# Gated delta-rule scan: state and output products in two alternating places, the query's product with the state moved behind the attention product

## The chip, the cores and the metric

The kernel runs on one core of one Trainium2 chip. The metric is the device time of one launch in microseconds, as a median over runs. All data are fp32. TensorE (PE in the profile) runs every fp32 matmul as two passes, so that one `nc.tensor.matmul` of the program shows as two MATMUL records and two LDWEIGHTS records.

## The reference, cut to what matters

The program computes two model blocks, one after the other: an RG-LRU layer followed by a gated DeltaNet layer, and then a layer with a long convolution and a state-space branch. The change touches the scan of the DeltaNet layer alone. Its recurrence over the chunks of a sequence is:

```
def step(state, inp):
    w_c, u_c, attn_c, q_c, k_c, e_c = inp
    v_new = u_c - einsum('bhcd,bhde->bhce', w_c, state)
    o_c = einsum('bhcd,bhde->bhce', q_c, state) + einsum('bhcm,bhme->bhce', attn_c, v_new)
    state = state * e_c[..., None, None] + einsum('bhcd,bhce->bhde', k_c, v_new)
    return state, o_c
```

There are 8 heads, 1024 tokens, and head size 128. Each chunk needs the state that the chunk before it left.

## The kernel before

The kernel cuts the 1024 tokens into 8 chunks of 128 (`NCH = 8`), so that every product of the scan is one 128x128x128 matmul. The 8 heads run one after the other: seven in a hardware loop, in which the threshold of each semaphore wait is computed in a register, and the last one written out behind it. A head first flips keys and queries, builds and inverts a triangular matrix for each chunk, and then scans its 8 chunks. While it does, TensorE also computes the four input projections of the next head ("fill" matmuls, 128x512, line 1279); in the last head the fills are the output projection of the heads that are done (line 1349).

The order is written by hand, one program for each engine; each engine takes its instructions strictly in that order and waits on semaphores. Within a chunk c these steps matter, named as in the code:

- **read** (PE, line 1447): keys times state, into place 0 of `R4`.
- **recall** (PE, line 1452, it has no mark of its own before): queries times state, into place 4 of `R5`.
- **delta** (DVE, line 1860): values minus the decayed read, into `delta[:, 0]`. It waits for read.
- **new** (PE, line 1455): the inverse times delta, into place 4 of `R4`. ACT copies it, scaled, to `delta[:, 1]` (line 1583).
- **mem** (PE, line 1459): keys times new, into place 0 of `R5`. DVE adds it to the decayed state and writes `memory` (line 1869).
- **o** (PE, line 1461): attention times new, into place 4 of `R4`, which new has used before. ACT copies it, scaled, to `o_tok` (line 1586); DVE then adds the scaled recall to it (line 1872; the tile is `part` or `part0` in the records).

One fill matmul stands between recall and new, and one between new and mem (two each in the last head). `R4` lies in PSUM banks 4 and 5 and `R5` in banks 6 and 7: places 0 to 3 of each in the first bank, 4 to 7 in the second. On DVE the order is: state of chunk c (1869), output of chunk c (1872), delta of chunk c + 1 (1860). In some chunks one more DVE instruction of 128x512 comes in: a join of projection products (line 1719) behind delta, and in the last head a sum (line 1732) ahead of delta. `memory` is one 128x128 tile before the change. Recall of chunk c + 1 waits until DVE and ACT are done with the output of chunk c, since it overwrites place 4 of `R5`.

When a head's scan is over, TensorE runs 4 more fills, flips the normed output (line 1370), runs the first 4 fills of the next head and flips its keys (line 1370 again), for which it waits for DVE's last step of the head (`y`, line 1889).

## Time and profile before

| what | value |
|---|---|
| median of 3 runs | 2160.57 us |
| lowest and highest run | 2154.43 and 2162.94 us |
| span of the profiled execution | 2150.7 us |
| PE busy in that span | 2070.0 us (96%) |
| DVE busy | 1364.1 us (63%) |
| ACT busy | 642.5 us (30%) |
| heads of the DeltaNet layer (from about 434 to 1191 us) | seven of 84.1 us and the last |

The profiled execution is one more execution, and its own device time is not among the three listed; its span runs from its first to its last instruction. The median of the runs lies 9.9 us above the span (2160.57 - 2150.7); what lies around the span is in that difference. The rows give start times in us from the span's start, and durations. A matmul's record includes the time in which its result drains while the next one already streams, so a start-to-start distance, not the duration, is what it costs in a row of matmuls.

### The profile page before, as it was taken

The numbers are of one execution on the slowest core, as the hardware profiler recorded it, in microseconds if no ns is written. First come the engines' busy times: TensorE is split into PE (matmuls) and PEld (weight loads), VectorE is DVE, ScalarE is ACT, GpSimd is POOL, SyncE is SP. The second block draws the span as 40 slices with busy tenths as digits, with TensorE's granted clock in tenths as the row PEclk, the third lists the DMA queues.
The fourth block names the chain that finished last, engine by engine and source line by source line (L and its number), as shares of the span: only waits on it lengthen the run. The fifth ranks groups of instructions, "written<-read, shape, count | busy, mean of one in ns | idle before, by whom it ended". The sixth has DMA issues, their size and how long they took to land. (4 is left out here: it accounts for less than half of the span.)

```text
span 2150.7 us, 20753 instructions
## 1 busy us (share of the span) xinstructions
PE 2070.0 (96%) x6898; PEld 1060.6 (49%) x6898; DVE 1364.1 (63%) x1918; ACT 642.5 (30%) x1063; POOL 234.5 (11%) x188
## 2 busy tenths in 40 slices
PE   6999999999999999999899899999999999999998
PEld 5444444446555556566555445554444444444443
DVE  4687753265746746647652578529999997534633
ACT  4345431323443434434311521012321111241021
POOL 0000001112212113122100400001000000003200
PEclk8999999999999999999999999999999999999999
DMA  9333389241111111111420316269722222334021
GB/s 342 110 109 100 116 272 236 89 92 35 47 29 37 38 37 37 24 36 43 147 41 1 108 59 120 74 189 250 173 59 75 68 73 69 103 103 137 20 98 59
DMA packets 243824, 207.17 MB, mean 96 GB/s; under 512 B 52204, under 2 KB 202785, under 8 KB 243745
## 3 DMA queue, kind: packets, MB, share of 16 engines
q1 hardware_dynamic: 213393, 157.25, 24.5%
q0 software_dynamic: 13056, 42.99, 8.2%
q10 hardware_dynamic: 17312, 6.10, 1.2%
q8 instruction: 38, 0.62, 0.1%
q14 instruction: 25, 0.20, 0.0%
HBM read 182.55 MB, written 60.33 MB: 113 GB/s over the span
## 5 line engine op out<-in xcount | busy, mean ns | idle before, releaser
L2300 PE MATMUL bank<-hT,ring 128*128 128x512 f32 x576 | 254.2, 592 | 0.0
L2300 PE MATMUL bank<-resid,ring 128*128 128x512 f32 x432 | 191.3, 592 | 0.0
L2300 PEld LDWEIGHTS bank<-hT,ring 128*128 128x128 f32 x576 | 109.5, 190 | 137.7 <-issue 136.7
L1279 PE MATMUL bank<-hT,ring 128*128 128x512 f32 x336 | 157.7, 595 | 1.8 <-ACT silu_z L1515 1.8
L3220 DVE SCALAR_TENSOR_TENSOR yT<-s_arena,yT 128x1024 f32<-128x1024 f32 x120 | 153.8, 1282 | 0.0
L3220 DVE SCALAR_TENSOR_TENSOR s_arena<-s_arena 128x1024 f32<-128x1024 f32 x112 | 143.5, 1282 | 0.0
L2272 PE MATMUL bank<-hT,ring 128*128 128x512 f32 x320 | 139.4, 594 | 0.0
L2300 PEld LDWEIGHTS bank<-resid,ring 128*128 128x128 f32 x432 | 82.1, 190 | 103.3 <-issue 102.3
L1869 DVE SCALAR_TENSOR_TENSOR memory<-memory,col_exp_last,bank 128x128 f32<-128x128 f32 x64 | 22.3, 348 | 153.7 <-PE bank L1459 153.7
L2272 PEld LDWEIGHTS bank<-hT,ring 128*128 128x128 f32 x320 | 60.2, 190 | 73.7 <-issue 73.4
L2345 PE MATMUL bank<-ssm_y,ring 128*128 128x512 f32 x192 | 83.4, 592 | 0.0
L1279 PEld LDWEIGHTS bank<-hT,ring 128*128 128x128 f32 x336 | 58.4, 191 | 49.9 <-issue 49.4
L1279 PE MATMUL bank<-resid,yT 128*128 128x512 f32 x168 | 82.5, 593 | 0.0
L2669 ACT ACTIVATE s_arena<-bank 128x512 f32<-128x512 f32 x54 | 32.2, 596 | 130.1 <-PE bank L2300 124.8
L640 PE MATMUL bank<-hT,ring 128*128 128x512 f32 x144 | 63.4, 595 | 0.3 <-DVE lru_arena L865 0.3
L1583 ACT ACTIVATE delta<-bank,gdn_stat 128x128 f32<-128x128 f32 x64 | 23.5, 367 | 128.5 <-PE bank L1455 128.5
L1349 PE MATMUL bank<-hT,yT 128*128 128x512 f32 x128 | 60.0, 593 | 0.0
L2345 PEld LDWEIGHTS bank<-ssm_y,ring 128*128 128x128 f32 x192 | 36.5, 190 | 45.9 <-issue 45.4
L3173 DVE TENSOR_TENSOR s_arena<-bank,s_arena 128x512 f32<-128x512 f32 x36 | 24.8, 688 | 53.6 <-PE bank L2300 53.6
L2595 PE MATMUL bank<-resid,s_arena 128*128 128x512 f32 x128 | 56.5, 593 | 1.1 <-DVE yT L3451 1.1
L685 PE MATMUL bank<-ada,yT 128*128 128x512 f32 x128 | 55.8, 593 | 0.7 <-issue 0.7
L685 PE MATMUL bank<-lru_arena,yT 128*128 128x512 f32 x128 | 56.1, 592 | 0.0
(585 smaller groups left out, 3671.7 us busy)
## 6 DMA issues: line engine op xcount, KB each, us to landing
ada<-in_ada_w SPq DMA_DIRECT2D x8, 2048.0 KB, 8.1
ring<-in_gdn_in_w SPq DMA_DIRECT2D x32, 512.0 KB, 4.1
ring<-in_w_in SPq DMA_DIRECT2D x54, 256.0 KB, 2.9
ab_U_sums<-in_w_in POOLq DMA_DIRECT2D x6, 2048.0 KB, 19.0
resid<-in_x SPq DMA_DIRECT2D x8, 1024.0 KB, 8.9
ring<-in_lru_in_w SPq DMA_DIRECT2D x16, 512.0 KB, 3.9
ring<-ab_U_sums SPq DMA_DIRECT2D x32, 256.0 KB, 3.0
lru_arena<-in_ada_w SPq DMA_DIRECT2D x6, 1024.0 KB, 12.5
```

Of the source, the lines that this page charges most:

```text
L640: last = nc.tensor.matmul(bank[:, to, :], w[:, k, :], v[:, k, :], start=(first and k == 0), stop=(k == KB - 1), skip_group_check=not (firs ...
L685: last = nc.tensor.matmul(bank[:, OUT_BANK[i], :], yT[:, k, t * P:(t + 1) * P], out_w[c][:, k, :], start=(k == 0), stop=(k == KT - 1))
L1279: last = nc.tensor.matmul(bank[:, to, :], w[:, k, :], v[:, k, :], start=(first and k == 0), stop=(k == KB - 1), skip_group_check=not only)
L1349: last = nc.tensor.matmul(bank[:, n % 4, :], yT[:, k, t * P:(t + 1) * P], w, start=(k == 0), stop=(k == KT - 2))
L1583: hd_act.mark(act.activation(delta[:, 1, :], R4[:, 4, :], ACT.Copy, scale=stat[:, 5, c:c + 1]), f"new{c}")
L2272: last = nc.tensor.matmul(bank[:, 2 * PAIR[name] + h, :], w[:, k, :], src[:, k, h * HALF:(h + 1) * HALF], start=(k == 0), stop=(k == kt - 1))
L2300: last = nc.tensor.matmul(bank[:, to, :], w[:, k, :], src[:, k, :], start=(start and k == 0), stop=(k == HK - 1), skip_group_check=not alone)
L2345: last = nc.tensor.matmul(bank[:, 2 * SINGLE_BANKS[name] + h, :], w[:, k, :], ssm_y[:, k, h * HALF:(h + 1) * HALF], start=(k == 0), stop=( ...
L2595: last = nc.tensor.matmul(bank[:, to, :], x[:, k, m, :], w[:, k, :], start=(start and k == 0), stop=(k == HK - 1), skip_group_check=not alone)
L2669: act_b.mark(act.activation(place, bank[:, PAIR_BANKS[name][2 if n == 2 else 0], :], ACT.Copy), f"{name}_kept{n}")
L3173: dve_b.mark(TT_(place, other, place, ALU.add), f"{name}_" + ("C11", "C12", None, "C22")[which])
L3220: dve_b.mark(dve.scalar_tensor_tensor(out=acc, in0=padded[:, p, j:j + S], scalar=taps[:, p, j:j + 1], in1=acc, op0=ALU.mult, op1=ALU.add), ...
```

## The change

`memory` becomes two tiles: chunk c reads `memory[:, c % 2]`, and the new state is written to `memory[:, (c + 1) % 2]`. The attention product o goes to place 5 or 6 of `R4` by turns, and recall to place 4 or 5 of `R5`. Recall is issued behind o, at the end of its chunk, and has a mark of its own. PE waits ahead of o for ACT's copy of the output of chunk c - 2, and ahead of recall for DVE's output step of chunk c - 2 (both only from c = 2 on); the wait for chunk c - 1 ahead of recall is gone. DVE waits for recall ahead of its output step.

```diff
-            memory = sb("memory", [P, P], scope)
+            memory = sb("memory", [P, 2, P], scope)
@@ PE
-                            hd_pe.mark(nc.tensor.matmul(R4[:, 0, :], kT[:, c, :], memory[:, :], start=True, stop=True), f"read{c}")
-                            if c:
-                                hd_dve.wait(pe, f"o{c - 1}", h)
-                                hd_act.wait(pe, f"o{c - 1}", h)
-
-                            nc.tensor.matmul(R5[:, 4, :], qT[:, c, :], memory[:, :], start=True, stop=True)
+                            hd_pe.mark(nc.tensor.matmul(R4[:, 0, :], kT[:, c, :], memory[:, c % 2, :], start=True, stop=True), f"read{c}")
                             fill(1, 2)
...
-                            hd_pe.mark(nc.tensor.matmul(R4[:, 4, :], attnT[:, c, :], delta[:, 1, :], start=True, stop=True), f"o{c}")
+                            if c >= 2:
+                                hd_act.wait(pe, f"o{c - 2}", h)
+                            hd_pe.mark(nc.tensor.matmul(R4[:, 5 + c % 2, :], attnT[:, c, :], delta[:, 1, :], start=True, stop=True), f"o{c}")
+                            if c >= 2:
+                                hd_dve.wait(pe, f"o{c - 2}", h)
+                            hd_pe.mark(nc.tensor.matmul(R5[:, 4 + c % 2, :], qT[:, c, :], memory[:, c % 2, :], start=True, stop=True), f"recall{c}")
@@ DVE
-                            hd_dve.mark(dve.scalar_tensor_tensor(out=memory[:, :], in0=memory[:, :], scalar=cols["exp_last"][:, h, c:c + 1],
+                            hd_dve.mark(dve.scalar_tensor_tensor(out=memory[:, (c + 1) % 2, :], in0=memory[:, c % 2, :], scalar=cols["exp_last"][:, h, c:c + 1],
                                                                  in1=R5[:, 0, :], op0=ALU.mult, op1=ALU.add), f"mem{c}")
+                            hd_pe.wait(dve, f"recall{c}", h)
                             hd_act.wait(dve, f"o{c}", h)
```

On TensorE, in the loop's heads, this is a stretch from the end of one chunk into the next before the change (names: `ck` keys, `cq` queries, `memory` state, `delta` the vectors, `buf_c` the inverse, `attnT` attention; L1279 is a fill):

```order
L1459 MATMUL bank<-delta,k_rest 128x128 [waits gdn_dve,gdn_act]
L1461 MATMUL bank<-delta,attnT 128x128
L58 REGISTER_ALU
L1447 MATMUL bank<-memory,ck 128x128 [waits gdn_dve]
L58 REGISTER_ALU
L58 REGISTER_ALU [waits gdn_dve]
L1452 MATMUL bank<-memory,cq 128x128 [waits gdn_act]
L1279 MATMUL bank<-resid,yT 128x512
L58 REGISTER_ALU
L1455 MATMUL bank<-delta,buf_c 128x128 [waits gdn_dve]
```

And the same stretch after it, from chunk 2 on:

```order
L1454 MATMUL bank<-delta,k_rest 128x128 [waits gdn_dve,gdn_act]
L58 REGISTER_ALU
L1458 MATMUL bank<-delta,attnT 128x128 [waits gdn_act]
L58 REGISTER_ALU
L1461 MATMUL bank<-memory,cq 128x128 [waits gdn_dve]
L58 REGISTER_ALU
L1447 MATMUL bank<-memory,ck 128x128 [waits gdn_dve]
L1279 MATMUL bank<-resid,ring 128x512
L58 REGISTER_ALU
L1450 MATMUL bank<-delta,buf_c 128x128 [waits gdn_dve]
```

The query's product stands ahead of the key's product now, and nothing is left between the key's product and the fill; two waits stand between the mem product and the query's product.

On DVE, from the state of one chunk to the delta of the next, one waiting instruction is new, ahead of the output step:

```order
 L1869 SCALAR_TENSOR_TENSOR memory<-memory,col_exp_last,bank 128x128
 L58 REGISTER_ALU
-L1872 SCALAR_TENSOR_TENSOR part<-bank,gdn_stat,part 128x128 [waits gdn_act]
+L58 REGISTER_ALU [waits gdn_pe]
+L1873 SCALAR_TENSOR_TENSOR part<-bank,gdn_stat,part 128x128 [waits gdn_act]
 L58 REGISTER_ALU
 L1860 ISA [waits gdn_pe]
```

The delta step still stands behind the output step.

## Rows read from the trace of the kernel before

**Rows 1.** The page: busy us and shares; clock in 40 slices; one group, idle before it

```profile
PE 2070.0 (96%) x6898; PEld 1060.6 (49%) x6898; DVE 1364.1 (63%) x1918; ACT 642.5 (30%) x1063; POOL 234.5 (11%) x188
...
PEclk8999999999999999999999999999999999999999
...
L1869 DVE SCALAR_TENSOR_TENSOR memory<-memory,col_exp_last,bank 128x128 f32<-128x128 f32 x64 | 22.3, 348 | 153.7 <-PE bank L1459 153.7
```

**Rows 2.** PE's waits, whole span: its longest line; us in total, times, longest us

```profile
PE bank L1447 <- DVE memory L1869: 16.6, 56, 0.3
```

**Rows 3.** Timeline of PE, loop's first head: start us, us, engine line tiles [idle before]

```profile
515.82 0.39 PE L1452 MATMUL bank<-memory,cq 128*128 128x128 f32 x2
516.04 1.02 PE L1279 MATMUL bank<-resid,yT 128*128 128x512 f32 x2
...
517.98 0.39 PE L1459 MATMUL bank<-delta,k_rest 128*128 128x128 f32 x2
518.20 0.39 PE L1461 MATMUL bank<-delta,attnT 128*128 128x128 f32 x2
518.90 0.49 PE L1447 MATMUL bank<-memory,ck 128*128 128x128 f32 x2 [0.31 <-DVE memory L1869]
519.51 0.48 PE L1452 MATMUL bank<-memory,cq 128*128 128x128 f32 x2
519.83 1.02 PE L1279 MATMUL bank<-resid,yT 128*128 128x512 f32 x2
520.69 0.38 PE L1455 MATMUL bank<-delta,buf_c 128*128 128x128 f32 x2
...
521.77 0.38 PE L1459 MATMUL bank<-delta,k_rest 128*128 128x128 f32 x2
```

**Rows 4.** Timelines of DVE and ACT in the same stretch

```profile
518.50 0.35 DVE L1869 SCALAR_TENSOR_TENSOR memory<-memory,col_exp_last,bank 128x128 f32<-128x128 f32 x1 [2.04 <-PE bank L1459]
519.03 0.35 DVE L1872 SCALAR_TENSOR_TENSOR part<-bank,gdn_stat,part 128x128 f32<-128x128 f32 x1 [0.18 <-ACT part L1586]
519.55 0.35 DVE L1860 SCALAR_TENSOR_TENSOR delta<-bank,col_neg_exp_g,v_tok 128x128 f32<-128x128 f32 x1 [0.18 <-PE bank L1447]
...
518.63 0.37 ACT L1586 ACTIVATE part<-bank,gdn_stat 128x128 f32<-128x128 f32 x1 [0.94 <-PE bank L1461]
```

**Rows 5.** Timeline of the second head: a weight load released by delta; a wait already met

```profile
600.20 0.35 DVE L1860 SCALAR_TENSOR_TENSOR delta<-bank,col_neg_exp_g,v_tok 128x128 f32<-128x128 f32 x1 [0.69 <-PE bank L1447]
600.61 0.19 PEld L1455 LDWEIGHTS bank<-delta,buf_c 128*128 128x128 f32 x1 [0.28 <-DVE delta L1860]
...
607.38 0.48 PE L1452 MATMUL bank<-memory,cq 128*128 128x128 f32 x2
...
607.70 1.02 PE L1279 MATMUL bank<-resid,ring 128*128 128x512 f32 x2
```

**Rows 6.** Timelines of PE and DVE, last head, one chunk into the next

```profile
1150.76 0.39 PE L1459 MATMUL bank<-delta,k_rest 128*128 128x128 f32 x2
...
1151.59 0.49 PE L1447 MATMUL bank<-memory,ck 128*128 128x128 f32 x2 [0.22 <-DVE memory L1869]
1152.27 0.49 PE L1452 MATMUL bank<-memory,cq 128*128 128x128 f32 x2 [0.20 <-DVE part L1872]
...
1152.73 0.35 DVE L1860 SCALAR_TENSOR_TENSOR delta<-bank,col_neg_exp_g,v_tok 128x128 f32<-128x128 f32 x1
```

**Rows 7.** Timelines of PE and DVE from a scan's end to the next head's keys

```profile
553.47 1.09 PE L1370 MATMUL bank<-ident,ck 128*128 128x128 f32 x8 [0.62 <-DVE yT L1889]
...
548.08 4.14 DVE L1658 SCALAR_TENSOR_TENSOR ck<-qkv_padded,vecs,ck 128x1024 f32<-128x1024 f32 x3
552.14 1.28 DVE L1889 SCALAR_TENSOR_TENSOR yT<-bank,vecs,silu_z 128x1024 f32 x1
```

**Rows 8.** PE ahead of the last head; then busy by window, with granted clock

```profile
1058.10 1.94 PE L1370 MATMUL bank<-ident,ck 128*128 128x128 f32 x8 [4.14 <-DVE yT L1889]
...
1056.00:1063.00 7.00, 4.90 (x23) 4.93 (x24) 7.00 (x6) 4.48 (x5) 3.24 (x1) 0.52 1.01 353
```

More of the change, by code:

```diff
@@ L1023, in block_program @@
             o_tok, o_normed = part0[:, :, :], AT
-            memory = sb("memory", [P, P], scope)
+            memory = sb("memory", [P, 2, P], scope)
             delta = sb("delta", [P, 2, P], scope)
             g_rows = delta[0:HEADS * NCH, 0, :]
-            fold_ab = memory[:, 0:2 * HEADS]
+            fold_ab = memory[:, 0, 0:2 * HEADS]
             g_dram = nc.dram_tensor("g_scratch", (HEADS * NCH, P), F32, kind="Internal").ap()
@@ L1041, in block_program @@
                           + [n for s in levels for n in halves(f"Y{s}") + (["v_flip"] if s == levels[0] else []) + halves(f"YT{s}") + (halves(f"F{s}") if s < 64 else [])]
-                          + [f"{n}{c}" for c in range(NCH) for n in ("read", "new", "mem", "o")] + ["o_flip"])
+                          + [f"{n}{c}" for c in range(NCH) for n in ("read", "new", "mem", "o", "recall")] + ["o_flip"])
             hd_act = Steps(sem("gdn_act"), ["k_sq", "decay", "q_silu", "q_sq", "k_rms", "v_silu"]
@@ L1585, in body @@
                             hd_pe.wait(act, f"o{c}", h)
-                            hd_act.mark(act.activation(o_tok[:, c, :], R4[:, 4, :], ACT.Copy, scale=stat[:, 1, c:c + 1]), f"o{c}")
+                            hd_act.mark(act.activation(o_tok[:, c, :], R4[:, 5 + c % 2, :], ACT.Copy, scale=stat[:, 1, c:c + 1]), f"o{c}")
                             if c:
@@ L1855, in body @@
                                 add_parts(7 + n, 8 + n)
-                        hd_pe.wait(dve, f"o{NCH - 1}", h, back=1)
-                        hd_dve.mark(dve.memset(memory[:, :], 0.0), "mem_zero")
+                        hd_pe.wait(dve, f"recall{NCH - 1}", h, back=1)
+                        hd_dve.mark(dve.memset(memory[:, 0, :], 0.0), "mem_zero")
                         for c in range(NCH):
@@ L1868, in body @@
                             hd_pe.wait(dve, f"mem{c}", h)
-                            hd_dve.mark(dve.scalar_tensor_tensor(out=memory[:, :], in0=memory[:, :], scalar=cols["exp_last"][:, h, c:c + 1],
+                            hd_dve.mark(dve.scalar_tensor_tensor(out=memory[:, (c + 1) % 2, :], in0=memory[:, c % 2, :], scalar=cols["exp_last"][:, h, c:c + 1],
                                                                  in1=R5[:, 0, :], op0=ALU.mult, op1=ALU.add), f"mem{c}")
+                            hd_pe.wait(dve, f"recall{c}", h)
                             hd_act.wait(dve, f"o{c}", h)
-                            hd_dve.mark(dve.scalar_tensor_tensor(out=o_tok[:, c, :], in0=R5[:, 4, :], scalar=stat[:, 3, c:c + 1],
+                            hd_dve.mark(dve.scalar_tensor_tensor(out=o_tok[:, c, :], in0=R5[:, 4 + c % 2, :], scalar=stat[:, 3, c:c + 1],
                                                                  in1=o_tok[:, c, :], op0=ALU.mult, op1=ALU.add), f"o{c}")
```

## The prediction

> **What bounds the kernel now.** I read the page first: PE is busy 96% of the span, and its clock reads 9 (90% or more) in all slices but the first [rows 1]. So time goes only if a hole in PE's stream goes, or PE gets less work; the change leaves PE its 5 small matmuls in each chunk. The second view is the list of PE's waits [rows 2]: its longest line is the key's product "read" (L1447), held 56 times by the state that DVE writes. 56 is 8 heads times chunks 1 to 7. But 16.6 us is not the whole hole, because a record covers the draining of a result. The whole is seen in start-to-start distances in the timeline [rows 3]. From mem to mem a chunk of the loop takes 521.77 - 517.98 = 3.79 us: mem to read 0.92, read to recall 0.61, recall to fill 0.32, fill to new 0.86, new to mem 1.08, which is new's 0.22 and the second fill's 0.86. A small matmul that follows another without a hole costs 0.22 (mem to o), so the distances 0.92, 0.61 and 0.32 hold the holes: 0.92 is mem and o (0.22 each) and 0.48 of waiting for DVE's state; 0.61 is read and 0.39 of waiting; 0.32 is recall and 0.10 of a start after a pause.
>
> Who releases recall? DVE's output step of the chunk before ends at 519.03 + 0.35 = 519.38, 0.13 ahead of recall at 519.51 [rows 3, 4]. DVE's state ends at 518.85, 0.05 ahead of read. So two releases follow each other: the state first, which the recurrence needs, and then the output step, which only frees a place in PSUM. In the last head the same pair is plain: read 1151.59, recall 1152.27, held by the output step [rows 6].
>
> **The change, part by part.**
>
> *Recall leaves the place between read and fill.* The wait for the output step of chunk c - 1 goes with it. The first fill can then start behind read alone. Read starts after a pause, as recall did, so I take recall's own distance to the fill for it: 0.32 (519.51 to 519.83). The distance from read to fill falls from 0.61 + 0.32 to 0.32.
>
> *Recall joins the end of its chunk.* Mem, o and recall now take 3 x 0.22 = 0.66, and read can't start until 0.92 after mem, since it waits for the state. The 0.48 hole takes recall's 0.22 in; 0.26 of it is left. In the last head the state is there 1151.59 - 1150.76 = 0.83 after mem [rows 6], still later than 0.66. So the recurrence sets read's start, as before, and recall there costs nothing.
>
> *New distance from mem to mem:* 0.92 + 0.32 + 0.86 + 0.22 + 0.86 = 3.18 instead of 3.79, **0.61 less**. In the last head read to recall is 1152.27 - 1151.59 = 0.68, and that goes.
>
> *What is late next.* With the first fill earlier, new could find its delta missing. Against the start of mem (517.98), delta runs from 1.57 to 1.92 [rows 4]. It is held by the end of read (0.92 + 0.49 = 1.41) and by DVE's output step (to 1.40) alike, and neither moves. The fill ends, and new can start, at 0.92 + 0.32 + 0.86 = 2.10. A weight load that delta releases comes 0.06 after delta's end (600.61 against 600.20 + 0.35) and takes 0.19 [rows 5]: 1.92 + 0.06 + 0.19 = 2.17. So new is between 0 and 0.07 late. I take 0: where the load was bare ahead of recall the matmul's second pass was only 0.10 behind its usual place, and with the load at 1.98 that fits into 2.10. The upper end, 0.07 in 49 chunks, is 3.4 us and goes into the range. In the last head two fills stand there, 1.72 us, and delta, even behind a sum, ends at 1153.08, 2.32 after mem; the fills last to 0.83 + 0.32 + 1.72 = 2.87. Nothing is late there.
>
> *Chunk 0* had no wait ahead of recall: 515.82 to 516.04, 0.22 [rows 3]. It moves from ahead of delta's path to the chunk's end and then fills the hole ahead of read 1. That is 0.22 less in each head. New of chunk 0 is ready for it: in the second head the load at 600.61 ends at 600.80, and the fill, 0.22 earlier than now, at about 600.77: 0 to 0.03 late.
>
> *Chunk 7* has no next read. Its recall puts 0.22 between o and the 4 fills at the head's end. Behind these PE waits 0.62 for DVE's last step `y` at the next head's keys, and DVE reaches `y` (552.14) straight out of its taps (548.08 to 552.22) [rows 7]; that chain starts at o, which recall follows. So the 0.22 comes out of the 0.62 in seven heads, and costs 0.22 in the last, where other work follows. Uncovered everywhere it would be 1.8 us.
>
> *The added waits.* PE's waits for chunk c - 2 are long met: DVE's output step of that chunk ended over one whole chunk earlier. What a met wait costs shows in two neighbours: recall to fill is 0.32 without a wait ahead of the fill (519.51, 519.83), and 607.70 - 607.38 = 0.32 with one [rows 3, 5]. So 0; the bound above is the 0.26 that is left ahead of read: only beyond it does a wait cost anything. DVE's new wait for recall has delta of chunk c + 1 queued behind it, and PE's new waits for that. Recall ends at 0.44 + 0.39 = 0.83 after mem; DVE's output step starts at 1.05, held by ACT's copy (0.65 to 1.02) [rows 4]. ACT is still last by 0.2.
>
> The Trainium skill, "Advanced Engine Details and Errata", Network/Comms, states 50 to 100 ns for a sequencer's reading of a semaphore. By it the two waits ahead of recall would put it up to 0.2 later, and the sum would shrink; the rows with a met wait show no such cost. This rule is the source of a rival below.
>
> *The state in two tiles* adds no instruction; DVE's state step keeps its shape (0.35). That PE reads one tile while DVE reads the same and writes the other is new in this trace: recall's two passes stream from 0.44 to 0.66, DVE's state step runs from 0.52. Bound: nothing below, since neither can get shorter; above, recall behind the whole state step, 0.43 later.
>
> *Sum:* 7 heads x 7 chunks x 0.61 = 29.9; last head 7 x 0.68 = 4.8; chunk 0, 8 x 0.22 = 1.8; last head's end, -0.22. Together **36.3 us**. The span goes from 2150.7 to 2114.4. The profiled execution's own device time isn't known; the runs' median lies 9.9 above its span, and I keep that: **2124.3 us**, 1.7% less.
>
> Outside the scan nothing else should answer. The weight loads for the next head are issued from points inside the fills and move with them; DVE idles 153.7 us ahead of its state steps alone, released by mem [rows 1], so it has room.
>
> **The rivals.**
>
> *A, a smaller gain: delta is late.* DVE's output step is held by recall instead of ACT, and delta behind it. Say each of the two added waits costs 0.1: recall then ends at 1.03, DVE starts 0.14 later (as the state step does: mem ends 518.37, DVE 518.50), at 1.17 instead of 1.05; delta ends at 2.04, its load at 2.29, and new is 0.19 late. That holds for the deltas behind chunks 2 to 6: 7 x 5 x 0.19 = 6.7 less, 2131. With recall held behind the whole state step (the 0.43 above), recall would end at 1.26, DVE's step start at 1.40, delta end at 2.27, its load at 2.52 and new 0.42 late: 49 chunks with 0.42 less, 20.6 us, 2145. The rows with a met wait speak against the first, and against the second only that both engines worked beside each other elsewhere. Chance of something from 2130 to 2146: 0.13.
>
> *B, no gain: the heads are paced by something else.* If DVE's chain at a head's end, or a load, did not move with the scan, PE's wait ahead of the keys (0.62) would grow by the 4.5 us that each head saves, and only the last head's gain would stay: 2156. Against it: DVE's chain follows the last chunk's output without a hole, and in the scan DVE idles most of the time. Chance of something from 2146 to 2171: 0.06.
>
> *C, slower: the output step of DVE becomes the scan's pace.* The place is the new DVE wait ahead of L1873. New may come 0.61 later than I say before a chunk is as long as it is now, that is, with DVE's output step at 1.05 + 0.54 = 1.59 (delta ends at 2.46, its load at 2.71); from there each 0.1 us costs 5.6 us over 56 chunks. It would need recall to end beyond 1.45 after mem instead of 0.83, and beyond 1.65 for 0.5% slower. In the trace no 128x128 matmul pair lasts over 0.49. Chance 0.03.
>
> *D, the clock.* PE's longest pause in the heads, 4.14 us ahead of the last one, is followed by a granted clock of 0.52, so mostly the 1.2 GHz level: the key flip takes 1.94 instead of 1.09 [rows 7, 8], 0.85 us more, and other work of that stretch likewise. After the change such pauses lie 30 us earlier; the fall can stay, go, or come at another pause. Both ways it is 1 to 3 us. The Trainium skill, "TensorE: Matmul & The Clock Gate", Part 1, says that how many matmuls run slow varies from run to run. No case of its own; it widens the others.
>
> **How the numbers follow.** Forecast (gain 30 to 38 us): 0.78; A: 0.13; B: 0.06; C: 0.03. The forecast's own range is 2116 to 2130: 2124.3, minus 2 for the clock and 6 for the spread of the runs (the lowest lies 6.1 below the median), plus 3.4 for the late new and 2 for the clock. To leave no more than 2 in 10 out I reach into A: 2115 to 2140. About 0.5% (10.8 us) is what a measurement of this kernel can tell from no change. Faster by more: 0.78 + 0.13 = 0.91 (both end below 2149.8); within: B's 0.06; slower: C's 0.03.
>
> **What would show it.** In the changed kernel's timeline: read to fill 0.32 where 0.93 was; mem to read still 0.92 (0.83 in the last head), with recall inside; mem to mem 3.18 in the loop and 4.8 in the last head; chunk 0 to chunk 1 0.22 shorter; the DVE output step released by ACT, not PE; the wait at the keys 0.4 instead of 0.62; each head of the loop 4.5 shorter. Delta's load late against the fill's end would show as a new line "L1450 held by DVE delta" in PE's waits. I am wrong if mem to read grows, if delta starts later than 1.57 after mem, or if the wait at the keys grows.

## The result, and the profile after

The changed kernel takes **2121.73 us** (median of 4 runs, 2120.38 to 2122.89); beside it, on the same chip, the kernel before takes 2157.82 (4 runs, 2154.43 to 2162.94). The ratio is 0.9838, 95% interval 0.982 to 0.9857: 36.1 us less, where 36.3 were forecast. One execution of the experiment e3 (5611 us) and one of the kernel before beside it (12333 us) were far slower than all others of their kernels and are left out of the medians and ratios below.

The page after. It answers to [rows 1]: busy us of each engine, and the group of DVE's state steps with its idle time.

```profile
PE 2058.8 (97%) x6898; PEld 1055.5 (50%) x6898; DVE 1364.1 (64%) x1918; ACT 642.7 (30%) x1063; POOL 235.3 (11%) x188
...
L1869 DVE SCALAR_TENSOR_TENSOR memory<-memory,col_exp_last,bank 128x128 f32<-128x128 f32 x64 | 22.2, 347 | 117.0 <-PE bank L1454 117.0
```

The instructions are the same in number (6898 on PE, 1918 on DVE). What fell is waiting: DVE's idle time ahead of its 64 state steps went from 153.7 to 117.0 us, since mem comes round sooner. That is 36.7 us, as much as the whole gain.

A chunk of the loop after the change, PE's timeline (start us, us, engine line tiles). New has moved to line 1450, mem to 1454, o to 1458, recall to 1461. It answers to [rows 3].

```profile
522.58 0.38 PE L1454 MATMUL bank<-delta,k_rest 128*128 128x128 f32 x2
522.80 0.39 PE L1458 MATMUL bank<-delta,attnT 128*128 128x128 f32 x2
523.02 0.39 PE L1461 MATMUL bank<-memory,cq 128*128 128x128 f32 x2
523.49 0.49 PE L1447 MATMUL bank<-memory,ck 128*128 128x128 f32 x2
523.82 1.02 PE L1279 MATMUL bank<-resid,ring 128*128 128x512 f32 x2
524.68 0.38 PE L1450 MATMUL bank<-delta,buf_c 128*128 128x128 f32 x2
524.90 1.02 PE L1279 MATMUL bank<-resid,ring 128*128 128x512 f32 x2
525.76 0.38 PE L1454 MATMUL bank<-delta,k_rest 128*128 128x128 f32 x2
```

Read it by starts. Mem to read is 523.49 - 522.58 = 0.91, as before, but mem, o and recall now fill 0.66 of it. Read to fill is 0.33, where read, the pause behind it and recall with its late start took 0.93. Fill to new is 0.86, the fill's own length. Mem to mem is 525.76 - 522.58 = **3.18**, forecast 3.18, before 3.79.

DVE and ACT beside it, and the weight load of new; in brackets the idle time and who ended it. It answers to [rows 4, 5].

```profile
523.09 0.35 DVE L1869 SCALAR_TENSOR_TENSOR memory<-memory,col_exp_last,bank 128x128 f32<-128x128 f32 x1 [1.18 <-PE bank L1454]
523.62 0.35 DVE L1873 SCALAR_TENSOR_TENSOR part<-bank,gdn_stat,part 128x128 f32<-128x128 f32 x1 [0.19 <-ACT part L1586]
524.13 0.35 DVE L1860 SCALAR_TENSOR_TENSOR delta<-bank,col_neg_exp_g,v_tok 128x128 f32<-128x128 f32 x1 [0.16 <-PE bank L1447]
...
523.23 0.37 ACT L1586 ACTIVATE part<-bank,gdn_stat 128x128 f32<-128x128 f32 x1 [0.94 <-PE bank L1458]
...
524.54 0.33 PEld L1450 LDWEIGHTS bank<-delta,buf_c 128*128 128x128 f32 x2 [0.53 <-DVE delta L1860]
```

The output step (L1873) starts 1.04 after mem and ACT releases it, not recall. Delta ends at 524.48, its load (the weight load of new) begins 0.06 later, and new still starts exactly when the fill is through, 0.14 behind the start of its load and ahead of the load's end. The state step starts 0.51 after mem (0.52 before): that PE reads one state tile while DVE reads it too and writes the other has cost nothing.

The last head, PE, one chunk into the next [rows 6], and PE at the next head's keys [rows 7]:

```profile
1120.18 0.38 PE L1454 MATMUL bank<-delta,k_rest 128*128 128x128 f32 x2
...
1120.62 0.39 PE L1461 MATMUL bank<-memory,cq 128*128 128x128 f32 x2
1121.00 0.49 PE L1447 MATMUL bank<-memory,ck 128*128 128x128 f32 x2
1121.33 1.88 PE L1349 MATMUL bank<-hT,yT 128*128 128x512 f32 x4
...
1124.99 0.38 PE L1454 MATMUL bank<-delta,k_rest 128*128 128x128 f32 x2
...
550.63 1.09 PE L1370 MATMUL bank<-ident,ck 128*128 128x128 f32 x8 [0.39 <-DVE yT L1890]
```

Mem to mem is 4.81 where 5.50 was; the wait at the keys is 0.39 where 0.62 was. The clock's fall ahead of the last head [rows 8] stayed: PE pauses 3.91 us, the key flip takes 1.94, and the window around it reads 0.57, mostly the 1.2 GHz level.

```profile
1028.34 1.94 PE L1370 MATMUL bank<-ident,ck 128*128 128x128 f32 x8 [3.91 <-DVE yT L1890]
...
1026.00:1034.00 8.00, 5.66 (x26) 5.46 (x27) 8.00 (x6) 4.48 (x5) 4.00 (x1) 0.57 1.01 339
```

**Where the span's difference lies.** The two profiled spans differ by less than the medians: 2150.7 against 2120.9, 29.8 us. Cut at three starts on PE (the first head's first read, the last head's first read, and the first product of the second block, line 2397 before, 2398 after), three profiles of the kernel before, one of e10 (below; its scan is that of before) and two of the changed kernel give, in us:

| profile | to first read | 7 heads | last head | rest | span |
|---|---|---|---|---|---|
| before | 515.5 | 625.5 | 53.2 | 956.4 | 2150.7 |
| e0_before_again | 517.3 | 625.6 | 53.2 | 957.9 | 2154.0 |
| e8_before_third | 514.1 | 625.5 | 53.2 | 961.5 | 2154.3 |
| e10_before_two_waits | 515.7 | 625.5 | 53.2 | 964.3 | 2158.8 |
| after | 517.2 | 594.2 | 48.4 | 961.1 | 2120.9 |
| e9_after_again | 514.0 | 594.7 | 48.5 | 960.8 | 2118.1 |

The two middle columns hold the effect: 31.3 + 4.8 = **36.1 us** in the first pair of profiles, and 30.8 + 4.7 = 35.5 with e9 in place of the first. The outer two vary by more than that between executions of one and the same program (514.1 to 517.3, 956.4 to 961.5); the part on the rest of the span comes back to them.

### The profile page after: what moved, and what is told of

The parts are those of the page before. It is cut to its first block and busy times, and to the rows that moved or that the text cites. A ratio compares the mean times of both kernels' runs of the same rounds, so it can differ in the third digit from the quotient of the medians.

```text
span 2120.9 us, 20796 instructions
## 1 busy us (share of the span) xinstructions
PE 2058.8 (97%) x6898; PEld 1055.5 (50%) x6898; DVE 1364.1 (64%) x1918; ACT 642.7 (30%) x1063; POOL 235.3 (11%) x188
## 5 line engine op out<-in xcount | busy, mean ns | idle before, releaser
L2301 PE MATMUL bank<-resid,ring 128*128 128x512 f32 x432 | 191.3, 592 | 0.0
L1279 PE MATMUL bank<-hT,ring 128*128 128x512 f32 x336 | 157.7, 595 | 1.8 <-ACT silu_z L1515 1.8
L1869 DVE SCALAR_TENSOR_TENSOR memory<-memory,col_exp_last,bank 128x128 f32<-128x128 f32 x64 | 22.2, 347 | 117.0 <-PE bank L1454 117.0
L1279 PEld LDWEIGHTS bank<-hT,ring 128*128 128x128 f32 x336 | 58.4, 190 | 49.9 <-issue 49.5
L1279 PE MATMUL bank<-resid,yT 128*128 128x512 f32 x168 | 82.5, 593 | 0.0
L3174 DVE TENSOR_TENSOR s_arena<-bank,s_arena 128x512 f32<-128x512 f32 x36 | 24.8, 690 | 53.2 <-PE bank L2301 53.2
L1279 PE MATMUL bank<-resid,ring 128*128 128x512 f32 x112 | 53.8, 593 | 0.0
```

Source lines behind the costliest of these rows:

```text
L1279: last = nc.tensor.matmul(bank[:, to, :], w[:, k, :], v[:, k, :], start=(first and k == 0), stop=(k == KB - 1), skip_group_check=not only)
L2301: last = nc.tensor.matmul(bank[:, to, :], w[:, k, :], src[:, k, :], start=(start and k == 0), stop=(k == HK - 1), skip_group_check=not alone)
L3174: dve_b.mark(TT_(place, other, place, ALU.add), f"{name}_" + ("C11", "C12", None, "C22")[which])
```

## The experiments

Each run stood beside runs of the kernel before on the same chip, and the ratios are to those, not to the first row: their median was 2153.70 us for e1, e2, e3 and e7, 2155.70 for e0, e4, e5 and e6, and 2159.37 for e8, e9 and e10. "Loop" and "last" are mem to mem in us. e8_before_third is a single execution of the kernel before (2156.29 us) and has no row.

| kernel | median (range), us | ratio (95%) | loop | last |
|---|---|---|---|---|
| before | 2157.82 (2154.43 to 2162.94) | 1 | 3.79 | 5.50 |
| changed | 2121.73 (2120.38 to 2122.89) | 0.9838 (0.982 to 0.9857) | 3.18 | 4.81 |
| e1_places_only | 2134.19 (2132.23 to 2136.7) | 0.9909 (0.9892 to 0.9925) | 3.41 | 5.03 and 5.11 to 5.17 |
| e2_one_psum_place | 2119.08 (2116.93 to 2119.84) | 0.9836 (0.9819 to 0.9852) | 3.18 | 4.81 |
| e3_one_state | 2147.84 (2145.67 to 2152.4) | 0.9971 (0.996 to 0.9982) | 3.63 | 5.26 |
| e7_recall_late | 2145.16 (2141.9 to 2147.99) | 0.9956 (0.994 to 0.9972) | 3.61 | 5.03 |
| e4_extra1 | 2124.72 (2122.06 to 2128.46) | 0.9869 (0.9852 to 0.9885) | 3.18 | 4.81 |
| e5_extra2 | 2129.45 (2127.46 to 2130.23) | 0.9886 (0.987 to 0.9903) | 3.28 | 5.00 |
| e6_four_waits | 2120.2 (2118.6 to 2123.07) | 0.9847 (0.983 to 0.9863) | 3.18 | 4.81 |
| e10_before_two_waits | 2155.12 (2152.19 to 2160.79) | 0.9984 (0.9973 to 0.9996) | 3.79 | 5.50 |
| e9_after_again | 2120.06 (2119.3 to 2122.49) | 0.9828 (0.9811 to 0.9844) | 3.18 | 4.81 |
| e0_before_again | 2157.05 (2152.68 to 2162.74) | 1.0011 (0.9999 to 1.0022) | 3.79 | 5.50 |

### Which part of the change carries it

**Recall where it was, places alternating.**

```diff
                             hd_pe.mark(nc.tensor.matmul(R4[:, 0, :], kT[:, c, :], memory[:, c % 2, :], start=True, stop=True), f"read{c}")
+                            if c >= 2:
+                                hd_dve.wait(pe, f"o{c - 2}", h)
+                            if c % 2:
+                                hd_act.wait(pe, f"o{c - 1}", h)
+                            hd_pe.mark(nc.tensor.matmul(R4[:, 7, :] if c % 2 else R5[:, 4, :], qT[:, c, :], memory[:, c % 2, :], start=True, stop=True), f"recall{c}")
```

> The alternation without the move: recall stands between read and fill as before; it writes by turns to a place of R5 (bank 7) and a place of R4 (bank 5), so that DVE's output step of the chunk before may still read its own bank while recall writes, and PE no longer waits for that step. My theory (two separate holes): mem to read stays 0.92, read to recall falls from 0.61 to 0.32 (read's start after a pause), recall to fill from 0.32 to 0.22, mem to mem 3.40 in the loop (before 3.79, changed kernel 3.18); in the last head 0.46 less per chunk than before. 49 x 0.39 + 7 x 0.46 = 22 us less than before, about 2136. Rival 'the wait for the output step was all of it, the place of recall is worth nothing': as fast as the changed kernel, about 2122. Rival 'the place is all of it': no gain, about 2158.

PE's timeline, mem, o, read, recall, fill, and the next mem:

```profile
521.69 0.38 PE L1459 MATMUL bank<-delta,k_rest 128*128 128x128 f32 x2
521.91 0.39 PE L1463 MATMUL bank<-delta,attnT 128*128 128x128 f32 x2
522.60 0.49 PE L1447 MATMUL bank<-memory,ck 128*128 128x128 f32 x2 [0.30 <-DVE memory L1871]
522.93 0.39 PE L1452 MATMUL bank<-memory,cq 128*128 128x128 f32 x2
523.15 1.02 PE L1279 MATMUL bank<-resid,ring 128*128 128x512 f32 x2
...
525.10 0.38 PE L1459 MATMUL bank<-delta,k_rest 128*128 128x128 f32 x2
```

Read to recall is 0.33 where 0.61 was, recall to fill 0.22 where 0.32 was: 0.38 of the 0.61 goes with the wait for the output step alone, without any move. The other 0.23 is recall itself, which still stands on the path here; in the changed kernel it lies in the hole ahead of read. The hole's line in PE's waits is unchanged in this kernel (16.6 us, 56 times, as [rows 2]), so it is not the state's wait that was shortened. In the last head the distance is 5.03 where recall is of an even chunk and 5.11 to 5.17 where it is of an odd one, since there a wait for ACT was left in.

To free recall from the output step at its old place, the second place had to lie in another PSUM bank. The Trainium skill, "PSUM — Partial Sum Buffer", section "PSUM bank collisions raise a hardware error", says that PE may not write a bank while another engine reads it on the same partitions, whatever the address. No run here shows that; by it the change's own alternation of neighbouring places in one bank could not let recall overlap DVE's reading of the place before.

**The move without the alternating places in PSUM.**

```diff
+                            if c:
+                                hd_act.wait(pe, f"o{c - 1}", h)
...
-                            hd_pe.mark(nc.tensor.matmul(R4[:, 5 + c % 2, :], attnT[:, c, :], delta[:, 1, :], start=True, stop=True), f"o{c}")
+                            hd_pe.mark(nc.tensor.matmul(R4[:, 4, :], attnT[:, c, :], delta[:, 1, :], start=True, stop=True), f"o{c}")
-                            if c >= 2:
-                                hd_dve.wait(pe, f"o{c - 2}", h)
-                            hd_pe.mark(nc.tensor.matmul(R5[:, 4 + c % 2, :], qT[:, c, :], memory[:, c % 2, :], start=True, stop=True), f"recall{c}")
+                            if c >= 1:
+                                hd_dve.wait(pe, f"o{c - 1}", h)
+                            hd_pe.mark(nc.tensor.matmul(R5[:, 4, :], qT[:, c, :], memory[:, c % 2, :], start=True, stop=True), f"recall{c}")
```

> The move and the two state tiles, but o in one place of R4 (that of new) and recall in one place of R5, with the waits for chunk c - 1 that this needs (for ACT's output copy ahead of new, for DVE's output step ahead of recall). My theory: these waits are met 1 us or more ahead at the new places, so the places in PSUM are worth nothing: mem to mem 3.18, about 2122, the same as the changed kernel within 3 us. Rival 'the alternating places carry part of the gain': mem to mem over 3.25, 2125 to 2145.

Loop 3.18 and last head 4.81, as in the changed kernel, and the intervals of the ratios (0.9819 to 0.9852, 0.982 to 0.9857) cover each other. Once recall is at the chunk's end, the output step of the chunk before ended some 2.2 us ahead of it (1.40 after its own mem, where recall starts 3.18 + 0.44 after that mem); the second places in PSUM buy nothing. (The wait for ACT stood ahead of recall before the change, but what it guards is place 4 of `R4`, which new overwrites; so it can stand ahead of new here.)

**The move with one state tile.** DVE's state step must then wait for recall.

```diff
-                            hd_pe.wait(dve, f"mem{c}", h)
-                            hd_dve.mark(dve.scalar_tensor_tensor(out=memory[:, (c + 1) % 2, :], in0=memory[:, c % 2, :], scalar=cols["exp_last"][:, h, c:c + 1],
-                                                                 in1=R5[:, 0, :], op0=ALU.mult, op1=ALU.add), f"mem{c}")
                             hd_pe.wait(dve, f"recall{c}", h)
+                            hd_dve.mark(dve.scalar_tensor_tensor(out=memory[:, 0, :], in0=memory[:, 0, :], scalar=cols["exp_last"][:, h, c:c + 1],
+                                                                 in1=R5[:, 0, :], op0=ALU.mult, op1=ALU.add), f"mem{c}")
```

> The move and the alternating places in PSUM, but one state tile: DVE may overwrite the state only behind recall, so its state step waits for recall instead of mem. My theory: the state step starts 0.45 later (recall ends 0.83 after mem begins, plus 0.14, so 0.97 instead of 0.52), and read with it: mem to read 1.37, mem to mem 3.63; the last head 5.26. Against before 7 x 1.3 + 1.9 = 11 us less, minus up to 2 for the head's end where DVE's chain starts later: about 2147 to 2150. Rival 'the second state tile is worth nothing, since PE has a hole there anyway': about 2122.

PE's mem, recall and read, and DVE's state and output steps:

```profile
521.51 0.39 PE L1454 MATMUL bank<-delta,k_rest 128*128 128x128 f32 x2
...
521.96 0.39 PE L1461 MATMUL bank<-memory,cq 128*128 128x128 f32 x2
522.88 0.49 PE L1447 MATMUL bank<-memory,ck 128*128 128x128 f32 x2 [0.53 <-DVE memory L1869]
...
522.48 0.35 DVE L1869 SCALAR_TENSOR_TENSOR memory<-memory,col_exp_last,bank 128x128 f32<-128x128 f32 x1 [1.62 <-PE bank L1461]
522.74 0.35 DVE L1872 SCALAR_TENSOR_TENSOR part<-bank,gdn_stat,part 128x128 f32<-128x128 f32 x1
```

The state step is released by recall, 0.97 after mem instead of 0.51, and mem to read is 1.37 instead of 0.91. Of the 0.61 only 0.16 is left. The second state tile is what makes the move pay: without it the recurrence itself waits for the query's product.

### How much room the hole has, and what the added waits cost

**One more product behind recall, then two** (the same 128x128x128 shape, into an unused place; their results are not used).

```diff
+                            hd_pe.mark(nc.tensor.matmul(R4[:, 1, :], qT[:, c, :], memory[:, c % 2, :], start=True, stop=True), f"extra{c}")
```

> The changed kernel with one more 128x128x128 matmul in each chunk, recall computed once more into an unused place (R4, place 1), between recall and the next read. My theory: 0.26 of the hole ahead of read is left, so 0.22 of PE work there is free in the loop: mem to read 0.92, mem to mem 3.18; in the last head 0.05 more per chunk. In all 0 to 1 us more than the changed kernel. Rival 'PE is the bound and every matmul costs its stream': 64 x 0.22 = 14 us more than the changed kernel.

> As the run with one more matmul, with two more. They stream until 1.10 after mem, past the state at 0.92: read starts at 1.10, without a pause ahead of it, fill at 1.32 instead of 1.24; delta 0.08 later, its load ends at 2.25 instead of 2.17 while the fill ends at 2.18. My theory: mem to mem 3.26 to 3.33, 0.17 more per chunk in the last head; 6 to 9 us more than the changed kernel. If every matmul cost its stream: 28 us more. If nothing is late at new even here: 3.26; if the load for new was already on the edge in the changed kernel: 3.33.

With one extra the loop stays at 3.18 and the heads at 79.6: four products, 0.88, still fit into 0.91. The 128 records more cost the scan nothing. In the last head I had expected 0.05 more per chunk: read does come 0.07 later there (0.89 after mem), but read to fill falls from 0.33 to 0.25, and mem to mem stays 4.81. With two, PE's timeline shows mem to read 522.23 - 521.12 = 1.11 and no pause ahead of read:

```profile
521.12 0.39 PE L1454 MATMUL bank<-delta,k_rest 128*128 128x128 f32 x2
...
522.23 0.39 PE L1447 MATMUL bank<-memory,ck 128*128 128x128 f32 x2
522.46 1.02 PE L1279 MATMUL bank<-resid,ring 128*128 128x512 f32 x2
...
524.40 0.38 PE L1454 MATMUL bank<-delta,k_rest 128*128 128x128 f32 x2
```

Read to fill is 0.23 here and 0.33 in the changed kernel: the pause's start costs 0.10, and it is given back when the pause is gone. So the second extra costs 0.20 - 0.10 = 0.10, and the chunk is 3.28. Of the 0.44 of the two extras, 0.24 fitted into the hole, for whose remainder 0.26 was forecast.

**Four more waits, already met, ahead of o.**

```diff
                             if c >= 2:
                                 hd_act.wait(pe, f"o{c - 2}", h)
+                                for again in range(2):
+                                    hd_act.wait(pe, f"o{c - 2}", h)
+                                    hd_dve.wait(pe, f"o{c - 2}", h)
```

> The changed kernel with four more waits on PE between mem and o, from chunk 2 on, all on counts that were reached a chunk ago: the price of a met wait, measured where nothing hides it but the wait of mem itself. By the rows of before (no difference between a fill with and without a met wait ahead of it) one such wait is free; four in a row should fill PE's sequencer for some 0.1 to 0.2 beyond what streams, so mem to o 0.3 to 0.4 instead of 0.22, with o, ACT's and DVE's output steps and delta later by the same, and 0 to 8 us more than the changed kernel. By the rate that the Trainium skill states for reading a semaphore (Advanced Engine Details and Errata, Network/Comms: 50 to 100 ns) mem to o would be 0.42 to 0.62 and the kernel 8 to 17 us slower.

```profile
524.64 0.38 PE L1454 MATMUL bank<-delta,k_rest 128*128 128x128 f32 x2
524.87 0.39 PE L1461 MATMUL bank<-delta,attnT 128*128 128x128 f32 x2
...
524.40 0.43 PEld L1454 LDWEIGHTS bank<-delta,k_rest 128*128 128x128 f32 x2 [0.42 <-ACT delta L1586]
524.77 0.30 PEld L1461 LDWEIGHTS bank<-delta,attnT 128*128 128x128 f32 x2
```

Mem to o is as without the added waits (0.22 on average over the loop; the 0.23 here is rounding), where I had expected 0.3 to 0.4. That does not make a met wait free. The load of mem, released by ACT, starts 0.24 ahead of mem, and between it and the load of o there are 0.37 us here (524.40 to 524.77), 0.35 in the changed kernel: five waits pass in that time, and only 0.02 of it shows, not in o's start. A price of up to some 0.07 each (0.37 / 5, an estimate) would stay hidden.

Where nothing hides it, the kernel before shows such a price. From the end of DVE's output step to recall's weight load, first in the loop and then in the last head:

```profile
519.50 0.30 PEld L1452 LDWEIGHTS bank<-memory,cq 128*128 128x128 f32 x2 [0.30 <-issue]
...
1151.87 0.35 DVE L1872 SCALAR_TENSOR_TENSOR part<-bank,gdn_stat,part 128x128 f32<-128x128 f32 x1 [0.33 <-ACT part L1586]
1152.27 0.30 PEld L1452 LDWEIGHTS bank<-memory,cq 128*128 128x128 f32 x2 [0.39 <-DVE part L1872]
```

In the loop the load starts 519.50 - 519.38 = 0.12 behind the end of the output step [rows 4], in the last head 1152.27 - 1152.22 = 0.05, and the load of read is 0.05 behind the state step too. These distances are the same in all 49 chunks of the loop and all 7 of the last head. In the loop PE takes the late wait (DVE) on a register instruction of its own and then the wait for ACT, met 0.4 us earlier, on the load; so a met wait and its instruction behind a late one cost 0.07. Which of the two instructions takes the time isn't separated. These 0.07 were part of the 0.39 of waiting ahead of recall. If the late wait came last in the kernel before, some 49 x 0.07 = 3.4 us might go by that alone; this is an estimate, and no run tried it.

The Trainium skill, "Advanced Engine Details and Errata", Network/Comms, gives 50 to 100 ns for reading a semaphore from a sequencer. Added to mem to o, four of them would have put o at 0.42 to 0.62 after mem by an estimate from that figure; the trace shows 0.22. As time on the sequencer the figure is not contradicted: the 0.07 lies within it, and five times its lower end, 0.25, fits into the 0.37.

The same in the kernel before, two met waits ahead of o:

```diff
+                            if c >= 2:
+                                hd_act.wait(pe, f"o{c - 2}", h)
+                                hd_dve.wait(pe, f"o{c - 2}", h)
                             hd_pe.mark(nc.tensor.matmul(R4[:, 4, :], attnT[:, c, :], delta[:, 1, :], start=True, stop=True), f"o{c}")
```

> The kernel before with two waits more on PE ahead of o, from chunk 2 on, on counts reached a chunk ago. It moves nothing in the scan (mem to mem 3.79) but alters the program's code like the variants did. Same time as before within 3 us. If the later wait for yT comes with any altered code, it shows 1.6 us or more here; if it comes with the earlier end of the scan, or from spread, under 0.5 or anything.

Loop 3.79, last head 5.50, mem to o 0.22: its scan is the kernel before's to 0.01 us. Its ratio, 0.9984 (0.9973 to 0.9996), excludes 1 by a hair. Its median lies 4.3 us below that of the kernel before beside it (2159.37 - 2155.12), with an unchanged scan; so a few us between two medians need not come from the scan.

### Rival C: what a late recall costs

**Recall of chunk c - 1 behind read of chunk c.** DVE's output step, and delta behind it, then wait for recall.

```diff
+                            if c:
+                                recall(c - 1)
                             fill(1, 2)
...
-                            hd_pe.mark(nc.tensor.matmul(R5[:, 4 + c % 2, :], qT[:, c, :], memory[:, c % 2, :], start=True, stop=True), f"recall{c}")
+                        recall(NCH - 1)
```

> The changed kernel with recall one matmul later: behind the read of the next chunk instead of ahead of it. Everything else as changed. A test of rival C (DVE's output step, which waits for recall, has delta queued behind it). By that mechanism: recall starts 1.24 after mem and ends at 1.63, DVE's output step runs from 1.77 to 2.12, delta from 2.29 to 2.64, its load ends at 2.89, mem to mem 3.97 in the loop, 0.18 more than before; in the last head, with its longer fills, 5.03, 0.46 less than before. In all 3 to 4 us slower than before, about 2161. If DVE had room and only PE's order counted: mem to mem 3.40, about 2136.

PE (mem, read, recall, fill, new, fill, mem), then DVE's output step and delta:

```profile
521.87 0.38 PE L1461 MATMUL bank<-delta,k_rest 128*128 128x128 f32 x2
...
522.78 0.49 PE L1452 MATMUL bank<-memory,ck 128*128 128x128 f32 x2 [0.31 <-DVE memory L1874]
523.11 0.39 PE L1450 MATMUL bank<-memory,cq 128*128 128x128 f32 x2
523.33 1.02 PE L1279 MATMUL bank<-resid,ring 128*128 128x512 f32 x2
524.29 0.49 PE L1457 MATMUL bank<-delta,buf_c 128*128 128x128 f32 x2
524.62 1.02 PE L1279 MATMUL bank<-resid,ring 128*128 128x512 f32 x2
525.48 0.38 PE L1461 MATMUL bank<-delta,k_rest 128*128 128x128 f32 x2
...
523.63 0.35 DVE L1878 SCALAR_TENSOR_TENSOR part<-bank,gdn_stat,part 128x128 f32<-128x128 f32 x1 [0.90 <-PE bank L1450]
523.90 0.34 DVE L1865 SCALAR_TENSOR_TENSOR delta<-bank,col_neg_exp_g,v_tok 128x128 f32<-128x128 f32 x1
```

The mechanism is there: the output step is held by recall (L1450), 1.76 after mem (1.77 expected), delta follows it, new is late. But the chunk is 3.61, not the 3.97 that the sum gave, and the kernel takes 2145.16 us, less than before, not the 2161 expected. The step that failed is delta's start: I let it follow the output step by 0.52, as everywhere in the scan, but those 0.52 hold delta's own wait for read. Here read was long done, and delta started 523.90 - 523.63 = 0.27 behind. New came 0.10 late and paid 0.11 for a start after a pause: 3.61 = 3.40 + 0.21.

### The rest of the span: a wait that came and went

In the profile of the changed kernel PE waits 3.60 us for the load of `yT` in the second block, hardly at all in the first profile of before (0.30). Did the change put it there? Three more profiles without edits, and e10:

> The kernel before, profiled once more, to see what moves by itself from one execution to the next: the clock's falls ahead of the scan and behind it, and the load of yT from its scratch, for which PE waited 3.6 us in the changed kernel and not before. If that wait comes from the change, it is absent here and in the next profiles of kernels without the change; if it is the load's own spread, it comes and goes in either. Same time as before.

> The kernel before, a third profile. In the two profiles of before so far PE waits 0.3 us or less ahead of the product of yT and s_arena (the long-convolution part, 140 us behind the last head), since the load of yT from its scratch lands in 12.1 to 12.5 us; in the changed kernel and in all seven variants so far it waits 1.6 to 6.9 us. If that is the load's own spread, this profile may show 2 to 5 us too; if the change, or anything that all the variants share, causes it, it shows under 0.5 again.

> The changed kernel once more, timed and profiled: 36 us less than before (ratio 0.983 to 0.984), mem to mem 3.18 and 4.81. The wait for yT: 1.6 to 7 us if it belongs to the variants, anything from 0 if it is spread.

The same product on PE, in turn in the first profile of before, e8, e10, the changed kernel, and e9:

```profile
1334.88 3.71 PE L2371 MATMUL bank<-yT,s_arena 128*64 128x128 f32 x64 [0.30 <-issue]
```

```profile
1336.89 5.38 PE L2371 MATMUL bank<-yT,s_arena 128*64 128x128 f32 x64 [2.16 <-issue]
```

```profile
1340.46 6.30 PE L2374 MATMUL bank<-yT,s_arena 128*64 128x128 f32 x64 [3.80 <-issue]
```

```profile
1305.15 3.71 PE L2372 MATMUL bank<-yT,s_arena 128*64 128x128 f32 x64 [3.60 <-DMA yT<-u_scratch]
```

```profile
1302.25 3.71 PE L2372 MATMUL bank<-yT,s_arena 128*64 128x128 f32 x64 [3.25 <-issue]
```

The unchanged kernel shows 2.16 in another execution (none at all in e0's), and 5.38 instead of 3.71 for the product, at a granted clock of 0.68. e10, whose scan is that of before, shows 3.80. So the wait does not need the earlier end of the scan. Whether it comes more often with any altered program text is not settled: three profiles of the unchanged text show 0.00, 0.30 and 2.16, and the ten of altered ones, e10 among them, 1.63 (e2) to 6.91 (e7). The stretch behind the scan shows the same picture: 956.4, 957.9 and 961.5 us in the three, 959.2 to 965.3 in the ten. By the question put ahead of e8 and e10, e8 speaks for spread and e10 for altered text.

What it means for the gain is read from the medians, beside the scans (the two middle columns, taken for each run):

| kernel | gain in the scan's stretches | gain in the medians |
|---|---|---|
| changed; e9 | 36.1; 35.5 | 36.1; 39.3 |
| e2, e6 | 35.6, 35.6 | 34.6, 35.5 |
| e1, e5 | 21.5, 29.5 | 19.5, 26.3 |
| e3, e4, e7 | 9.8, 35.4, 13.3 | 5.9, 31.0, 8.5 |
| e10 | 0.0 | 4.3 |

In the changed kernel's two pairs nothing is given back. The medians of the others miss their scans by up to 5 us, most of them downwards, and e10 by 4.3 upwards. No run separates the causes of these few us; a difference in medians of that size says nothing here about the scan, and the experiments are read by their mem to mem distances.

## Why the prediction was right, point by point

- **The bound.** PE's stream paced by holes in the scan: right. All of the gain is in the scan's stretches, and DVE's idle time ahead of the state shows it a second time (153.7 to 117.0).
- **Read to fill** 0.32 forecast, 0.33 measured. **Mem to read** forecast unchanged at 0.92 and 0.83, measured 0.91 and 0.82. **Mem to mem** forecast 3.18 in the loop and 4.8 in the last head, measured 3.18 and 4.81. What let it be exact is that each distance was taken between starts of neighbours in rows, the pause's cost included. e1 and e3 show the two halves: 0.38 goes with the wait alone, and the move without the second state tile brings 0.16.
- **Recall in the hole.** 0.48 of waiting, 0.22 of it taken, 0.26 left: e4's extra product (0.22) fits; two (0.44) put read 0.20 later, so 0.24 was free.
- **What is late next.** I took 0 between 0 and 0.07. Delta's load began 0.06 behind delta, as the row of the second head had it, and new was not late. The bound of 3.4 us in the range was not needed: it let new wait for its load's end, and new starts ahead of that (524.68, the load's first record running from 524.54 for 0.19). That delta is held by the end of read and by the output step alike was misread: only read held it, as e7 shows (delta 0.27 behind the output step's start).
- **Chunk 0.** 0.22 less in each head: in the second head read 0 to read 1 was 602.99 - 599.63 = 3.36, and is 3.14 now. Each head of the loop is 79.60 where 84.09 was, 4.49 less; forecast 7 x 0.61 + 0.22 = 4.49.
- **Chunk 7 and the keys.** The wait went from 0.62 to 0.39, and recall's 0.22 was covered, as forecast.
- **The added waits.** 0 in mem to read and mem to mem, as forecast, but not because a met wait is free: PE's stand under cover of running matmuls, and DVE's new wait stands ahead of the one that is held (ACT), not behind it. The prediction's own two figures, recall 0.13 behind the output step and read 0.05 behind the state, held the 0.07 that such a wait costs in the open, and it passed over them. ACT still releases the output step.
- **Rivals.** A (late delta) needed a cost of a met wait or of two engines on the state's tiles; neither reached the output step, which starts 1.04 after mem (1.05 before). B (heads paced by something else): each head moved with its scan. C's mechanism exists, but it was priced too dear: with the output step at 1.76, beyond the 1.59 from which C said a chunk would be longer than 3.79, e7 has 3.61. Delta's 0.52 behind the output step was the wrong term. D: the fall ahead of the last head stayed, the rest of the clock differs from execution to execution.
- **A term that was wrong** is what lies around the span. I read 9.9 us from the listed median and the profiled span. The profiled executions' own times show 2.0: the changed kernel's is 2122.89 with a span of 2120.9, e8's 2156.29 with 2154.3. The other 7.9 was that execution being a fast one beside the median of three. Since the sum was in effect taken off the median of the runs (2160.57 - 36.3), it did no harm; made against the profiled execution's own time it would have given 2150.7 + 2.0 - 36.3 = 2116.4.
- **Luck.** The 36.3 is a sum of rounded terms (36.2 without rounding), and the scan's stretches give 36.1 and 35.5; that agreement is the mechanism's. That the medians agree to 0.2 is in part luck: with e9 their difference is 39.3. The 2.6 us by which the time itself was missed (2124.3 - 2121.73) are about the 2.75 by which the three listed runs of before lay above the four measured beside the changed kernel (2160.57 - 2157.82).

## What to carry to other kernels

Where a serial chain leaves a hole on the busiest engine, look for an operation of the same step that stands on the path only because its operand or its place will be overwritten, and move it into the hole; what must be doubled is the operand that the chain overwrites (here the state: 0.45 us a chunk), not the result's place (here 0.00, once the product stands in the hole). Split such a distance into the wait, the operation and the start after the pause, each from two starts in the timeline, and check what remains of the hole before anything is put in. A difference of two spans has to be cut into stretches before it is explained: two profiles of the same program can differ by 5 us in a stretch that no edit touched (956.4 and 961.5 here).

## What the runs showed of the hardware

- Already met waits on PE's queue, up to five in a row between two small matmuls, did not move the second one's start (0.22 either way, e6), though its weight load came 0.02 later. Behind a wait that ends late, a met wait with its instruction cost 0.07 (0.12 instead of 0.05 from the releasing step's end to the weight load, kernel before).
- A DVE step of 128x128 with its inputs ready starts 0.27 behind the step ahead of it (e7; 522.74 - 522.48 = 0.26 in e3), less than that step's record of 0.35. Released by PE's read it starts 0.51 to 0.52 behind in the same place. Spacing read from a stretch with waits can't be used where the wait is gone.
- A small fp32 matmul, in two passes, takes 0.22 in a stream, and 0.32 or 0.33 to the next start if it comes after a pause, with its weight load starting together with it; with the load 0.14 ahead, as for new in the changed kernel, it takes 0.22. This 0.10 comes back when the pause is filled (e5).
- PE can stream a state tile while DVE reads the same tile and writes its neighbour: the state step took 0.35 us and started 0.51 after mem, as before.
